# Router logits from the raw turned X of a two-layer MoE block, with the norm's factors folded into the router weights

## The chip, the cores and the metric

The kernel runs on one core of a Trainium2 chip. TensorE (PE) multiplies matrices, VectorE (DVE) and ScalarE (ACT) work on rows, GpSimd (POOL) and SyncE (SP) here mostly issue DMAs. The metric is the device time of one execution in microseconds (us), lower is better.

## The reference, cut to what matters

The whole program computes two layers of attention plus a hierarchical MoE (`first_block`), then a second block. All is float32. The part that the change touches stands between attention and the experts, once per layer:

```python
x = x + gt_a * (o @ w_o[i])                        # x: 256 rows; layer 0 also has 256 context rows xc
hf = _modulate(_rmsnorm(x, g_ffn[i]), sh_f, sc_f)  # h * (1 + scale) + shift
# _rmsnorm: x * rsqrt(mean(x*x) + eps) * g
# _hier_moe(tokens, ...):
p_grp = softmax(h @ w_group + b_group)             # 4 groups
lg = h @ w_router + b_router                       # 32 experts
# the best group, the best 2 of its 8 experts, and then the rows of h go to these experts
```

So 36 logits per token are wanted, and the rows h themselves, which the experts read.

## The kernel before, in words

A layer treats 4 tiles of 128 rows (layer 0: two of x, two of the context) or 2 (layer 1). `BATCHES` cuts them for the router: tiles (0, 1) and (2, 3) in layer 0, (0) and (1) in layer 1.

The loop after attention (`for tile in range(tiles)`, the W_o loop) does for each tile, in this order on PE: `wo_part` with column half 0 (8 products of 128x128 by 128x512; each is two matmul instructions in the trace, L1043), then for the tile before it `norm_turn` (8 transposes of its normed rows, L648) and, halfway through column half 1, `logits` (8 products with the 36 router columns `WRT`, L1053). DVE takes each half out with `out_part` (gate multiply L2269, add to X L2272). ACT makes the mean square and its root from the new X (`norm_sums`: L1420, L1422). DVE then makes the reciprocal (L1838) and the normed and modulated rows h (`modulated`: L1844, L1846). These rows `Hf` have two uses: POOL stores them to `h_d` in HBM (L2912), and PE turns them; ACT and DVE each copy one half of the turned tile into `HT` (L1409, L1851), from which `logits` reads.

When a batch's logits are there, DVE runs `route` (L1997 to L2025: top group, top two experts, counts), PE sums the counts (`positions`, L1061 and L1063), DVE makes slots and one-hot rows (`slots`, `map_rows`: L2042 to L2073), PE multiplies them into the slot map (`slot_map`, L787) and DVE hands the map over (`map_out`, L2079, a mark at L2081). POOL then gathers the first experts' input rows from `h_d` (L2925); it issues this gather behind waits for the map and for all stores of h (`s_hst`). PE turns them (L804) and the expert products start (L816).

Weights come through a ring of 6 slots of 2 MB, with one more slot in layer 0 and two more in layer 1, loaded by SP in a fixed order; each load waits until the last reader of its slot is done (L3037, L3035). Four facts of that order matter. The extra slot's first load (`in_w_up`) waits for the end of attention. Two loads wait for the two halves of w_o. The next (`in_w_gate`) takes the slot of the shift and scale rows, so it waits for the last `s_h`, which is what L1846 of the last tile counts up. All later ones wait for expert products.

ACT issues one DMA at the end of attention: the gains `g_ffn`, broadcast to 128 partitions (`VG`, L1517, 512 KB). DVE needs them for `scales` (L1814), after tile 0. All DMAs counted by `s_pre` are waited for together.

Of the kernel before, what the change touches and what calls it, by code (L numbers as in the profile page):

```python
# [110 lines left out]
def build(nc, t, out):  # L111

    ctx = ExitStack()
    with ctx:
# [3 lines left out]
        def sem(name):  # L118
            return ctx.enter_context(nc.semaphore(name))
# [68 lines left out]
        BRT = cut(20384, 36)  # L188
        SINK = cut(20424, HEADS)
        CROWS = cut(SCR, P, parts=7 * KD)  # L190

        STAGE = [cut(a, 512) for a in (21504, 21504, SCR, 21504, 21504, 21504)]
        QUADS = [(layer, c) for layer in range(2) for c in range(0, 12, 4)]
# [190 lines left out]
        s_silus = sem("silu_of_z")  # L384
        s_pos2 = sem("final_gain_and_positions")
        s_out = sem("out_stored")

        block = ctx.enter_context(nc.Block())

# [220 lines left out]
        def _(pe):  # L610
# [342 lines left out]
            def hT(tile, k):  # L953
                return HT[:, k, tile * P:(tile + 1) * P]

            for layer in range(2):
# [89 lines left out]
                def logits(tile):  # L1046
                    a, b = [x for x in BATCHES[layer] if x[0] <= tile < x[1]][0]
                    if tile == a:
                        pe.wait_ge(s_psd, so_far(s_ps))
                    pe.wait_ge(s_outA, turned[tile][0])  # L1050
                    pe.wait_ge(s_outD, turned[tile][1])
                    for k in range(KD):
                        ins = nc.tensor.matmul(banks[6][:, (tile - a) * 36:(tile - a) * 36 + 36], hT(tile, k), WRT[:, k, :],  # L1053
                                               start=(k == 0), stop=(k == KD - 1))
                    if tile == b - 1:
                        ins.then_inc(s_lg, 1)

                def positions(a, b):
# [7 lines left out]

                turned.clear()
                for tile in range(tiles):
                    pe.wait_ge(s_otaken, GROUPS_BEFORE[layer] + KV * (tile + 1))
                    u = unit("D")  # L1070
                    wo_part(u, tile, 0, range(KD)).then_inc(s_unitD, 1)
                    if tile == tiles - 1:
                        release(n0, "D")
                    early = batch_ending(layer, tile - 2)
                    if early:
                        positions(*early)
                    if tile:
                        norm_turn(tile - 1, Hf[(tile - 1) % 2])
                        turned.append((count["A"], count["D"]))
                    u = unit("D")  # L1080
                    wo_part(u, tile, 1, range(KD // 2))
                    if tile:
                        logits(tile - 1)
                    wo_part(u, tile, 1, range(KD // 2, KD)).then_inc(s_unitD, 1)
                    if tile == tiles - 1:
                        release(n1, "D")
                early = batch_ending(layer, tiles - 2)
                if early:
                    positions(*early)
                norm_turn(tiles - 1, Hf[(tiles - 1) % 2])  # L1090
                turned.append((count["A"], count["D"]))
# [306 lines left out]
        def _(act):  # L1398
# [40 lines left out]
            def rows_to_ht(tiles):  # L1439
                for tile in tiles:  # L1440
                    u = take()
                    copy_out(HT[:, 0:4, tile * P:(tile + 1) * P], u[:, :].rearrange("p (k n) -> p k n", k=4))

            act.wait_ge(s_x, 16)
            for layer in range(2):
# [63 lines left out]
                for s in range(len(units) + 4):  # L1509
# [4 lines left out]
                    if 0 <= s - 1 < len(units):  # L1514
                        scaled(s - 1)
                act.wait_ge(s_o, GROUPS_AFTER[layer])
                act.dma_start(VG, t["g_ffn"][layer].partition_broadcast(P)).then_inc(s_pre, 16)  # L1517
                for tile in range(tiles):
                    if tile >= 1:
                        rows_to_ht([tile - 1])  # L1520
                    norm_sums([tile], X)
                rows_to_ht([tiles - 1])
# [217 lines left out]
        def _(dve):  # L1740
# [65 lines left out]

            def scales(layer, kinds):

                dve.wait_ge(s_pre, due(s_pre, 16))
# [25 lines left out]
            def modulated(layer, tile):  # L1835
# [4 lines left out]
                h = Hf[tile % 2]  # L1840
                if tile >= 2:
                    dve.wait_ge(s_hst[tile % 2], due(s_hst[tile % 2], 16))
                va, vb = ffn_rows(layer, tile // LAT)
                V.scalar_tensor_tensor(h, X(tile), rstd[:, tile:tile + 1], va, ALU.mult, ALU.mult).then_inc(s_v, one(s_v))  # L1844
                dve.wait_ge(s_v, so_far(s_v))
                V.tensor_tensor(h, h, vb, ALU.add).then_inc(s_h, one(s_h))  # L1846
                dve.wait_ge(s_h, so_far(s_h))

            def half_out(tile):
                u = take()  # L1850
                V.tensor_copy(HT[:, 4:8, tile * P:(tile + 1) * P], u[:, :].rearrange("p (k n) -> p k n", k=4)).then_inc(s_outD, one(s_outD))  # L1851

            def rope(tile, h0, h1, dst, tmp):

# [120 lines left out]
            def route(layer, a, b):  # L1975
# [9 lines left out]
                def first(dst, values, top, order, w, tmp):  # L1985
# [8 lines left out]
                    dve.wait_ge(s_v, so_far(s_v))  # L1994

                dve.wait_ge(s_lg, due(s_lg))
                V.tensor_tensor(lg, banks[6][:, 0:36 * n].rearrange("p (t e) -> p t e", t=n), bc(BRT.unsqueeze(1), P, n, 36),  # L1997
                                ALU.add).then_inc(s_v, one(s_v))
# [214 lines left out]
            for layer in range(2):  # L2213
# [51 lines left out]
                def out_part(tile, c):  # L2265
                    gate = GATE[tile // LAT]
                    cs = slice(c * 512, (c + 1) * 512)
                    u = take()
                    V.tensor_tensor(RES, u[:, :], gate[:, cs], ALU.mult).then_inc(s_outD, one(s_outD))  # L2269
                    dve.wait_ge(s_outD, so_far(s_outD))  # L2270
                    done = s_v if c == 0 else s_xr
# [3 lines left out]
                for tile in range(tiles):  # L2275
                    out_part(tile, 0)
                    early = batch_ending(layer, tile - 2)
                    if early:
                        slots(layer, *early)
                        map_rows(*early)  # L2280
                    if tile:
                        half_out(tile - 1)
                    done = batch_ending(layer, tile - 1)
                    if done:
                        route(layer, *done)
                    out_part(tile, 1)
                    if tile == tiles - 1:
                        V.memset(mark(), 0.0).then_inc(s_par_free, one(s_par_free))
                    if tile == 0:
                        scales(layer, tiles // LAT)  # L2290
# [4 lines left out]
                early = batch_ending(layer, tiles - 2)  # L2295
                if early:
                    slots(layer, *early)
                    map_rows(*early)
                half_out(tiles - 1)
                route(layer, *BATCHES[layer][1])  # L2300
# [847 lines left out]
```

## Time and profile before

| | |
|---|---|
| three runs | 2111.34 us median (2108.47 to 2114.01) |
| profiled execution | 2110.83 us, of which the span is 2109.0 us |
| PE busy | 1971.9 us (93% of the span) |
| DVE, ACT, POOL busy | 1062.7, 405.5, 118.9 us |
| DMA | 584.23 MB, mean 277 GB/s |
| chain that ended last | PE 76%, DMA 13%, DVE 8%, ACT 2% |

The page's strips show PE nearly full from end to end, with two dips in which also the granted clock of PE falls, one after each W_o loop. Times in the rows below are from the span's start. The first number of a timeline row is its start and the second its length; the bracket at its end is how long the engine was idle before it and what ended that.

### The profile page before, as it was taken

The numbers are of one execution on the slowest core, as the hardware profiler recorded it, in microseconds if no ns is written. First come the engines' busy times: TensorE is split into PE (matmuls) and PEld (weight loads), VectorE is DVE, ScalarE is ACT, GpSimd is POOL, SyncE is SP. The second block draws the span as 40 slices with busy tenths as digits, with TensorE's granted clock in tenths as the row PEclk, the third lists the DMA queues.
The fourth block names the chain that finished last, engine by engine and source line by source line (L and its number), as shares of the span: only waits on it lengthen the run. The fifth ranks groups of instructions, "written<-read, shape, count | busy, mean of one in ns | idle before, by whom it ended". The sixth has DMA issues, their size and how long they took to land.

```text
span 2109.0 us, 20648 instructions
## 1 busy us (share of the span) xinstructions
PE 1971.9 (93%) x8057; PEld 888.9 (42%) x8057; DVE 1062.7 (50%) x1974; ACT 405.5 (19%) x836; POOL 118.9 (6%) x168
## 2 busy tenths in 40 slices
PE   6999987999999999988799988898999999999999
PEld 2445443333333333454333333333445554445554
DVE  1257545445554445674433222322767665666665
ACT  2146411000000002162100000000312230212230
POOL 1001002000000000000100000000100000100000
PEclk9999997999999999999799999999999999999999
DMA  9267435999999998455599999999733333723431
GB/s 356 98 232 264 184 127 223 416 425 426 427 427 427 426 427 329 173 210 188 220 425 426 427 425 427 425 426 424 268 114 120 120 120 120 255 101 115 140 134 65
DMA packets 95043, 584.23 MB, mean 277 GB/s; under 512 B 10044, under 2 KB 14436, under 8 KB 62044
## 3 DMA queue, kind: packets, MB, share of 16 engines
q1 hardware_dynamic: 84400, 559.96, 65.7%
q0 software_dynamic: 10256, 21.86, 3.1%
q8 instruction: 67, 1.10, 0.2%
q10 hardware_dynamic: 288, 1.05, 0.2%
q14 instruction: 32, 0.26, 0.0%
HBM read 589.05 MB, written 4.26 MB: 281 GB/s over the span
## 4 chain that ended last, share of the span: by engine, by line
PE 76%; DMA 13%; DVE 8%; ACT 2%; SPq 1%; issue 1%; DVEq 0%; POOLq 0%; ACTq 0%
PE bank L816 25%; PE bank L1144 11%; PE bank L821 6%; DMA ring<-in_w_gate 6%; PE bank L975 6%; DMA ring<-in_w_up 4%; PE bank L1223 4%; PE bank L1159 3%; PE bank L1120 3%; PE bank L1043 2%; PE bank L766 2%; PE bank L663 2%; PE bank L754 2%; PE bank L804 1%; DMA ring<-in_w_qkv 1%
## 5 line engine op out<-in xcount | busy, mean ns | idle before, releaser
L816 PE MATMUL bank<-ring,big 128*64 128x512 f32 x2464 | 684.7, 602 | 25.7 <-DMA ring<-in_w_gate 10.0
L816 PEld LDWEIGHTS bank<-ring,big 128*64 128x64 f32 x2464 | 217.7, 138 | 387.3 <-issue 374.2
L2165 DVE TENSOR_TENSOR big<-bank,big 128x512 f32<-128x512 f32 x192 | 131.6, 685 | 252.3 <-PE bank L821 251.5
L816 PE MATMUL bank<-big 128*64 128x512 f32 x512 | 227.5, 594 | 0.0
L1144 PE MATMUL bank<-ring,big 128*128 128x512 f32 (+1 forms) x448 | 205.3, 600 | 5.3 <-DVE ring L2548 3.3
L821 PE MATMUL bank<-big 128*128 128x512 f32 x360 | 180.1, 610 | 0.0
L975 PE MATMUL bank<-ring,big 128*128 128x512 f32 x320 | 141.8, 602 | 3.8 <-ACT big L1435 2.0
L1144 PEld LDWEIGHTS bank<-ring,big 128*128 128x128 f32 x448 | 82.6, 193 | 93.9 <-issue 92.8
L2369 DVE TENSOR_TENSOR big<-big,bank 128x512 f32<-128x512 f32 x32 | 22.0, 687 | 184.5 <-PE bank L816 184.5
L975 PEld LDWEIGHTS bank<-ring,big 128*128 128x128 f32 x320 | 61.2, 193 | 80.0 <-issue 74.7
L816 PEld LDWEIGHTS bank<-big 128*64 128x64 f32 x512 | 68.6, 137 | 58.9 <-issue 58.9
L821 PEld LDWEIGHTS bank<-big 128*128 128x128 f32 x360 | 59.4, 191 | 78.3 <-issue 78.3
L2170 DVE TENSOR_TENSOR xl<-xl,big 128x512 f32<-128x512 f32 x128 | 88.7, 693 | 4.4
L1529 ACT ACTIVATE big<-bank 128x512 f32<-128x512 f32 x32 | 19.1, 597 | 362.3 <-PE bank L804 362.3
L1223 PE MATMUL bank<-ring,big 128*128 128x512 f32 x192 | 83.6, 593 | 1.5 <-ACT big L1409 1.5
L1409 ACT ACTIVATE big<-bank 128x512 f32<-128x512 f32 (+2 forms) x66 | 36.3, 568 | 252.5 <-PE bank L975 115.8
L1043 PE MATMUL bank<-ring,big 128*128 128x512 f32 x192 | 84.6, 595 | 0.0
L1561 ACT ACTIVATE big<-bank 128x512 f32<-128x512 f32 x32 | 19.1, 597 | 326.2 <-PE bank L816 326.2
L1144 PE MATMUL bank<-ring 128*128 128x512 f32 (+1 forms) x176 | 79.2, 590 | 0.0
L2386 DVE COPY big<-bank 128x512 f32<-128x512 f32 x32 | 22.1, 692 | 106.7 <-PE bank L816 106.7
L2920 POOL MEMSET big<- 128x1024 f32 x32 | 30.3, 952 | 678.4 <-PE bank L804 666.9
L663 PE MATMUL bank<-ring,small 128*32 128x512 f32 x384 | 54.1, 657 | 7.5 <-DMA ring<-in_w_ada 7.5
(443 smaller groups left out, 2380.8 us busy)
## 6 DMA issues: line engine op xcount, KB each, us to landing
ring<-in_w_gate SPq DMA_DIRECT2D x52, 2048.0 KB, 17.9
ring<-in_w_up SPq DMA_DIRECT2D x51, 2048.0 KB, 21.2
ring<-in_w_down SPq DMA_DIRECT2D x51, 2048.0 KB, 20.5
ring<-in_w_ada SPq DMA_DIRECT2D x24, 2048.0 KB, 10.4
ring<-in_w_in SPq DMA_DIRECT2D x24, 2048.0 KB, 7.9
big<-in_w_up SPq DMA_DIRECT2D x9, 2048.0 KB, 21.3
big<-in_w_down SPq DMA_DIRECT2D x9, 2048.0 KB, 21.6
big<-in_w_gate SPq DMA_DIRECT2D x8, 2048.0 KB, 19.2
```

The lines of the kernel that those rows point to most:

```text
L663: ins = nc.tensor.matmul(u[32 * i:32 * i + 32, :], cW[:, 2 * k:2 * k + 32], w[:, (4 * (k % 2) + i) * 512:(4 * (k % 2) + i + 1) * 512], sta ...
L754: ins = nc.tensor.transpose(banks[4 + r][:, o * P:(o + 1) * P], src, ident)
L816: ins = nc.tensor.matmul(bank[half * CAP:(half + 1) * CAP, :], lhs[:, k, half * CAP:(half + 1) * CAP], slot_cols(slots[half], k * step + c ...
L821: return nc.tensor.matmul(bank, OHW[layer][j][:, (u // 2) * P:(u // 2 + 1) * P], YS[j][:, (u % 2) * 512:(u % 2 + 1) * 512], start=True, st ...
L975: ins = nc.tensor.matmul(u[:, :], hT(tile, k), w[:, k, :], start=(k == 0), stop=(k == KD - 1))
L1043: ins = nc.tensor.matmul(u[:, :], hT(tile, k), wo[c][:, k, :], start=(k == 0), stop=(k == KD - 1))
L1120: ins = nc.tensor.matmul(u[:, 0:cols], HT2[:, k, tile * P:(tile + 1) * P], w[:, 0:KD * cols].rearrange("p (k n) -> p k n", k=KD)[:, k, :], ...
L1144: ins = nc.tensor.matmul(u[:, 0:cols], a[:, k, :], b[:, k, :], start=(k == 0 and (name not in ADDS_TO or (g in (IN_PAIRS, FIRST) and name ...
L1159: ins = nc.tensor.matmul(u[:, 0:n], HT2[:, k, tile * P:(tile + 1) * P], w[:, k, :], start=(k == 0), stop=(k == KD - 1))
L1223: ins = nc.tensor.matmul(u[:, :], YT[n % 2][:, k, tile * P:(tile + 1) * P], w[:, k, c * 512:(c + 1) * 512], start=(k == 0), stop=(k == 3))
L2165: return r, V.tensor_tensor(r, bank, GATE[tile // LAT][:, half * 512:(half + 1) * 512], ALU.mult)
L2170: return V.tensor_tensor(x, x, r, ALU.add)
```

## The change

X itself is turned, not h. With X the updated rows, r their reciprocal root, the logits are r * (X @ M) + B, where M is W with each row multiplied by g * (1 + scale), and B is shift @ W + bias.

- ACT issues small DMAs ahead of `VG`: the shift and scale rows of each stream (2 streams in layer 0) as 16 rows of 128, and g_ffn as 8 rows of 128. They count on `s_pre` as `VG` does.
- PE, in tile 0 after 4 of the 8 steps of unit 0, waits for all DMAs on `s_pre` and turns these rows (`columns_turn`). It then makes shift @ W (`shift_product`) and spreads it over the partitions (`shift_rows`); ACT copies each out.
- DVE makes M (`router_weights`) and B (`router_bias`) during tile 0.
- PE turns X of the tile before after 2 steps of unit 0 (`x_turn`) and makes its logits after 6. Of the last tile the first half is turned inside unit 1, the second behind it.
- ACT copies both halves of the turned tile.
- `route` begins with one multiply-add of PSUM, r and B per tile.
- The last tile's h is finished (`shifted_rows`, the adding of the shift, which counts `s_h`) behind the last `route`. In layer 1 `slots` of batch 0 stands ahead of the last `out_part`.

```diff
@@ PE
+                def columns_turn():
+                    pe.wait_ge(s_pre, due(s_pre, 16 * (2 + streams)))
+                    n = 16 * streams + KD
+                    nc.tensor.transpose(unit("A")[:, 0:n], MROWS[0:n, :], ident[0:n, 0:n]).then_inc(s_unitA, 1)
...
+                def shift_product():
+                    pe.wait_ge(s_outA, count["A"])
...
+                        ins = nc.tensor.matmul(u[0:36, 0:streams], WRT[:, k, :], MCOL[:, k:k + 16 * streams:16], start=(k == 0), stop=(k == KD - 1))
...
+                def x_turn(tile, half):
...
+                        ins = nc.tensor.transpose(u[:, k * P:(k + 1) * P], X(tile)[:, c:c + P], ident)
...
-                    wo_part(u, tile, 0, range(KD)).then_inc(s_unitD, 1)
...
+                    if tile == 0:
+                        wo_part(u, tile, 0, range(4))
+                        columns_turn()
+                        wo_part(u, tile, 0, range(4, KD)).then_inc(s_unitD, 1)
+                        shift_product()
+                    else:
+                        wo_part(u, tile, 0, range(2))
+                        pe.wait_ge(s_xr, X_BEFORE + tile)
+                        x_turn(tile - 1, 0)
+                        x_turn(tile - 1, 1)
+                        wo_part(u, tile, 0, range(2, 6))
+                        logits(tile - 1)
+                        wo_part(u, tile, 0, range(6, KD)).then_inc(s_unitD, 1)
...
+                    wo_part(u, tile, 1, range(4))
+                    if tile == 0:
+                        shift_rows()
+                    if final:
+                        pe.wait_ge(s_xh, layer + 1)
+                        x_turn(tile, 0)
+                    wo_part(u, tile, 1, range(4, 7))
+                    if final and batch_ending(layer, tiles - 2):
+                        positions(*batch_ending(layer, tiles - 2))
+                    wo_part(u, tile, 1, range(7, KD)).then_inc(s_unitD, 1)
...
-                norm_turn(tiles - 1, Hf[(tiles - 1) % 2])
-                logits(tiles - 1)
+                logits(tiles - 1, 0)
+                pe.wait_ge(s_xr, X_BEFORE + tiles)
+                x_turn(tiles - 1, 1)
+                logits(tiles - 1, 1)
@@ ACT
+                act.wait_ge(s_mod, (128, 256)[layer])
+                for s in range(streams):
+                    act.dma_start(MROWS[16 * s:16 * s + 16, :], mod_d[layer, s, 3 * D:5 * D].rearrange("(k p) -> k p", p=P)).then_inc(s_pre, 16)
+                act.dma_start(MROWS[16 * streams:16 * streams + KD, :], t["g_ffn"][layer].rearrange("(k p) -> k p", p=P)).then_inc(s_pre, 16)
                 act.dma_start(VG, t["g_ffn"][layer].partition_broadcast(P)).then_inc(s_pre, 16)
...
+                    if tile == tiles - 1:
+                        rows_to_ht(tile, 0)
+                    act.wait_ge(s_xr, due(s_xr))
+                    nc.scalar.activation(junk[:, :], X(tile), ACT.Square, accum_out=ss[:, tile:tile + 1]).then_inc(s_a, one(s_a))
+                    if tile == tiles - 1:
+                        rows_to_ht(tile, 1)
+                    act.wait_ge(s_a, so_far(s_a))
+                    nc.scalar.activation(ss[:, tile:tile + 1], ss[:, tile:tile + 1], ACT.Sqrt, scale=1.0 / D, bias=eps).then_inc(s_ss, 1)
@@ DVE
+                for tile in range(a, b):
+                    bias = BRM[:, 36 * (tile // LAT):36 * (tile // LAT) + 36]
+                    ins = V.scalar_tensor_tensor(LG[:, tile, :], banks[6][:, 36 * (tile - a):36 * (tile - a) + 36], rstd[:, tile:tile + 1], bias,
+                                                 ALU.mult, ALU.add)
...
-                    modulated(layer, tile)
+                    if between:
+                        map_rows(*between)
+                    scaled_rows(layer, tile)
+                    if not final:
+                        shifted_rows(layer, tile)
+                route(layer, *BATCHES[layer][1])
+                shifted_rows(layer, tiles - 1)
                 last_use[at["rows", layer]] = (s_h, so_far(s_h))
```

First place: ACT at the end of layer 0's attention (`big<-in_g_ffn 128x1024` is `VG`). Before:

```order
L1482 ACTIVATE big<-bank 128x2x256 x2
L1517 DMA big<-in_g_ffn 128x1024
L1420 ACTIVATE junk,small<-xl 128x1024
L1422 ACT_TABLE_LOAD
L1422 ACTIVATE small<-small 128x1
```

Now:

```order
L1535 ACTIVATE big<-bank 128x2x256 x2
L1573 DMA big<-mod_d 16x128 x2
L1574 DMA big<-in_g_ffn 8x128
L1575 DMA big<-in_g_ffn 128x1024
L1463 ACTIVATE big<-bank 128x40
L1463 ACTIVATE big<-bank 36x2
L1463 ACTIVATE big<-bank 128x72
L1584 ACTIVATE junk,small<-xl 128x1024
```

`VG` is now the fourth DMA on ACT instead of the first (the third in layer 1), and three copies out of PSUM stand ahead of the first square.

Second place: PE at the head of the same W_o loop (`wo_part` is L1043 before and L1047 now). Before:

```order
L766 MATMUL bank<-big 64x256 x8
L1043 MATMUL bank<-ring,big 128x512 x24
L648 MATMUL bank<-cst,big 128x128 x8
L1043 MATMUL bank<-ring,big 128x512 x4
L1053 MATMUL bank<-big 128x36 x8
```

Now:

```order
L770 MATMUL bank<-big 64x256 x8
L1047 MATMUL bank<-ring,big 128x512 x4
L1056 MATMUL bank<-cst,big 128x40
L1047 MATMUL bank<-ring,big 128x512 x4
L1064 MATMUL bank<-big 36x2 x8
L1047 MATMUL bank<-ring,big 128x512 x4
L1072 MATMUL bank<-cst,big 128x36 x2
L1047 MATMUL bank<-ring,big 128x512 x6
L1081 MATMUL bank<-cst,xl 128x128 x8
```

L1056 waits for the four ACT DMAs and has only 4 steps of W_o ahead of it; 24 unbroken steps became 4, 4, 4 and 6 until the first tile is turned.

Third place: DVE behind the last update of X in layer 0. Before:

```order
L2272 TENSOR_TENSOR xc<-xc,big 128x512
L2288 MEMSET small 128x1
L1838 RECIPROCAL small<-small 128x1
L1844 SCALAR_TENSOR_TENSOR big<-xc,small,ring 128x1024
L1846 TENSOR_TENSOR big<-big,ring 128x1024
L1851 COPY big<-bank 128x4x128
L1997 TENSOR_TENSOR big<-bank,big 128x72
```

Now (ahead of the route's rows, and behind them):

```order
L2363 TENSOR_TENSOR xc<-xc,big 128x512
L2381 MEMSET small 128x1
L1907 RECIPROCAL small<-small 128x1
L1912 SCALAR_TENSOR_TENSOR big<-xc,small,ring 128x1024
L2087 SCALAR_TENSOR_TENSOR big<-bank,small,big 128x36 x2
...
L2116 TENSOR_TENSOR big<-big 128x32 x2
L1918 TENSOR_TENSOR big<-big,ring 128x1024
L2133 TENSOR_TENSOR big<-bank,cst 128x64
```

The copy out of PSUM is gone, and the add that finishes h moved from ahead of the route to behind it.

## Rows read from the trace of the kernel before

**Rows 1.** Windows: busy us of PE, PEld, DVE, ACT, POOL; clock; DMA share; GB/s
```profile
238.00:305.00 67.00, 64.42 (x210) 32.57 (x206) 30.71 (x68) 7.41 (x13) 1.65 (x3) 1.00 0.26 95
500.00:600.00 100.00, 100.00 (x420) 37.91 (x418) 50.41 (x75) 8.37 (x14) 7.78 (x8) 1.00 1.01 427
1200.00:1300.00 100.00, 88.10 (x392) 34.65 (x389) 28.18 (x44) 7.53 (x13) 6.18 (x7) 1.00 1.01 425
```

**Rows 2.** Timeline of layer 0's W_o loop and of what follows its last unit
```profile
238.52 20.87 PE L1043 MATMUL bank<-ring,big 128*128 128x512 f32 x48
...
264.12 1.87 PE L1053 MATMUL bank<-big 128*128 128x36 f32 x16
...
299.89 1.95 PE L1053 MATMUL bank<-big 128*128 128x36 f32 x16 [1.60 <-DVE big L1851]
...
305.38 0.69 DVE L2269 TENSOR_TENSOR big<-bank,big 128x512 f32<-128x512 f32 x1 [5.64 <-PE bank L1043]
...
308.01 0.29 ACT L1422 ACTIVATE small<-small 128x1 f32<-128x1 f32 x1
...
309.86 1.22 DVE L1846 TENSOR_TENSOR big<-big,ring 128x1024 f32<-128x1024 f32 x1
...
311.14 1.97 PE L648 MATMUL bank<-cst,big 128*128 128x128 f32 x8 [5.79 <-DVE big L1846]
...
317.69 0.23 DVE L1997 TENSOR_TENSOR big<-bank,big 128x72 f32<-128x72 f32 x1 [3.79 <-PE bank L1053]
```

**Rows 3.** Timeline of layer 0 from the end of the last route to the gather
```profile
323.50 0.74 PE L1061 MATMUL bank<-big,cst 128*128 128x96 f32 x2 [4.16 <-DVE big L2025]
...
331.02 0.06 DVE L2081 MEMSET small<- 128x1 f32 x1
...
332.01 1.06 POOL L2925 DMA_INDIRECT big<-h_d,slot_tok  x1 [12.45 <-DVE small L2081]
```

**Rows 4.** DMAs at the end of layer 0's attention; then KB, us to landing
```profile
238.62 0.38 ACTq L1517 DMA_DIRECT2D big<-in_g_ffn  x1
239.12 0.33 SPq L3037 DMA_DIRECT2D big<-in_w_up  x1
...
big<-in_w_up SPq DMA_DIRECT2D x1, 2048.0 KB, 9.1
big<-in_g_ffn ACTq DMA_DIRECT2D x1, 512.0 KB, 4.5
```

**Rows 5.** PE after a wait of 4 us in layer 1's attention, and that window
```profile
898.71 1.11 PE L985 MATMUL bank<-cst,big 128*128 128x128 f32 x4 [4.00 <-DVE big L1882]
...
896.00:904.00 8.00, 4.46 (x20) 2.18 (x20) 4.12 (x9) 1.49 (x2) 0.00 (x0) 0.57 1.01 380
```

**Rows 6.** Stores of h: issue of layer 0's last, landings at 260, 311 and 1002
```profile
311.38 0.53 POOL L2912 DMA_DIRECT2D h_d<-big  x1 [16.85 <-DVE big L1846]
...
h_d<-big POOLq DMA_DIRECT2D x1, 512.0 KB, 2.9
...
h_d<-big POOLq DMA_DIRECT2D x1, 512.0 KB, 9.5
...
h_d<-big POOLq DMA_DIRECT2D x1, 512.0 KB, 9.8
```

**Rows 7.** Layer 1: the DMAs at attention's end, the last unit, route and gather
```profile
963.51 0.34 ACTq L1517 DMA_DIRECT2D big<-in_g_ffn  x1
964.00 0.33 SPq L3037 DMA_DIRECT2D big<-in_w_up  x1
...
995.60 0.69 DVE L2269 TENSOR_TENSOR big<-bank,big 128x512 f32<-128x512 f32 x1
...
1008.86 0.20 DVE L1997 TENSOR_TENSOR big<-bank,big 128x36 f32<-128x36 f32 x1 [3.78 <-PE bank L1053]
...
1013.95 0.69 PE L1061 MATMUL bank<-big,cst 128*128 128x64 f32 x2 [4.29 <-DVE big L2025]
...
1020.70 1.08 POOL L2925 DMA_INDIRECT big<-h_d,slot_tok  x1 [9.97 <-DVE small L2081]
```

More of the change, by code:

```diff
@@ L190, in build @@
         CROWS = cut(SCR, P, parts=7 * KD)
+        WRM = [cut(4096 + 288 * s, 288, KD, 36) for s in range(2)]
+        MROWS, MCOL = cut(4672, P), cut(4800, 40)
+        BCOL, BRM = cut(4840, 2), cut(4844, 72)
         STAGE = [cut(a, 512) for a in (21504, 21504, SCR, 21504, 21504, 21504)]
@@ L1044, in wo_part @@
                     return ins
-                def logits(tile):
+                streams = tiles // LAT
+                def columns_turn():
+                    pe.wait_ge(s_pre, due(s_pre, 16 * (2 + streams)))
+                    n = 16 * streams + KD
+                    nc.tensor.transpose(unit("A")[:, 0:n], MROWS[0:n, :], ident[0:n, 0:n]).then_inc(s_unitA, 1)
+                    marks["columns", layer] = count["A"]
+                def shift_product():
+                    pe.wait_ge(s_outA, count["A"])
+                    u = unit("A")
+                    for k in range(KD):
+                        ins = nc.tensor.matmul(u[0:36, 0:streams], WRT[:, k, :], MCOL[:, k:k + 16 * streams:16], start=(k == 0), stop=(k == KD - 1))
+                    ins.then_inc(s_unitA, 1)
@@ new lines, in shift_rows @@
+                def shift_rows():
+                    pe.wait_ge(s_outA, count["A"])
+                    u = unit("A")
+                    for s in range(streams):
+                        ins = nc.tensor.matmul(u[:, 36 * s:36 * s + 36], BCOL[0:36, s:s + 1].to_broadcast([36, P]), ident[0:36, 0:36],
+                                               start=True, stop=True)
+                    ins.then_inc(s_unitA, 1)
+                def x_turn(tile, half):
+                    u = unit("A")
+                    for k in range(4):
+                        c = (4 * half + k) * P
+                        ins = nc.tensor.transpose(u[:, k * P:(k + 1) * P], X(tile)[:, c:c + P], ident)
+                    ins.then_inc(s_unitA, 1)
+                    turned.append(count["A"])
@@ L1047, in logits @@
+                X_BEFORE = (NT, 3 * NT)[layer]
+                def logits(tile, half=None):
                     a, b = [x for x in BATCHES[layer] if x[0] <= tile < x[1]][0]
-                    if tile == a:
+                    if tile == a and half != 1:
                         pe.wait_ge(s_psd, so_far(s_ps))
[L1050 to L1053, printed above, removed]
+                    pe.wait_ge(s_outA, turned[2 * tile + (0 if half == 0 else 1)])
+                    for k in range(KD) if half is None else range(4 * half, 4 * half + 4):
+                        ins = nc.tensor.matmul(banks[6][:, (tile - a) * 36:(tile - a) * 36 + 36], hT(tile, k), WRM[tile // LAT][:, k, :],
@@ L1054, in logits @@
                                                start=(k == 0), stop=(k == KD - 1))
-                    if tile == b - 1:
+                    if tile == b - 1 and half != 0:
                         ins.then_inc(s_lg, 1)
@@ L1437, in modulated_to_ht, with rows_to_ht @@
                     ins.then_inc(s_outA, 1)
[L1439 to L1442, printed above, removed]
+            def rows_to_ht(tile, half):
+                u = take()
+                copy_out(HT[:, 4 * half:4 * half + 4, tile * P:(tile + 1) * P], u[:, :].rearrange("p (k n) -> p k n", k=4))
             act.wait_ge(s_x, 16)
@@ L1833, in modulated_half, with scaled_rows @@
                 ins.then_inc(s_outD, one(s_outD))
-            def modulated(layer, tile):
+            def scaled_rows(layer, tile):
                 dve.wait_ge(s_ss, due(s_ss))
@@ L2275, in _ @@
                 for tile in range(tiles):
+                    final = tile == tiles - 1
+                    if batch_ending(layer, tile - 2):
+                        slots(layer, *batch_ending(layer, tile - 2))
+                        map_rows(*batch_ending(layer, tile - 2))
                     out_part(tile, 0)
[L2277 to L2285, printed above, removed]
+                    if tile == 0:
+                        router_weights(layer, tiles // LAT)
+                    if batch_ending(layer, tile - 1):
+                        route(layer, *batch_ending(layer, tile - 1))
+                    between = final and batch_ending(layer, tiles - 2)
+                    if between:
+                        slots(layer, *between)
                     out_part(tile, 1)
-                    if tile == tiles - 1:
+                    if final:
                         V.memset(mark(), 0.0).then_inc(s_par_free, one(s_par_free))
                     if tile == 0:
+                        router_bias(layer, tiles // LAT)
                         scales(layer, tiles // LAT)
@@ L2292, in _ @@
                             dve.wait_ge(s_mod, 128)
-                    modulated(layer, tile)
-                last_use[at["rows", layer]] = (s_h, so_far(s_h))
[L2295 to L2300, printed above, removed]
+                    if between:
+                        map_rows(*between)
[4 more added lines that the diff above has]
+                shifted_rows(layer, tiles - 1)
+                last_use[at["rows", layer]] = (s_h, so_far(s_h))
                 slots(layer, *BATCHES[layer][1])
```

71 lines of the change are left out of this document (40 added, 31 removed).

## Prediction

> **What bounds the kernel now.** I read the windows first, to see which engine fills each stage. In layer 0's W_o loop PE is busy 64.42 of 67 us at full clock [rows 1], so there whatever PE does more, or waits for, is paid. In the expert stages PE is busy for the whole of a window of layer 0 at 427 GB/s, and 88 of 100 us in layer 1 at 425 GB/s, where the DMAs pace it [rows 1]. Both stages start from the same point: the ring is full, the next load waits for the first expert product, and that waits for the gather. So the expert stages, bound by PE or by DMA, move as a block with the gather, and what the change is worth is read from two moments, the gather at 332.01 [rows 3] and the one at 1020.70 [rows 7].
>
> Then the timeline up to each gather. W_o costs 20.87/48 = 0.435 us an instruction, and logits 1.87 us a tile [rows 2]. After the last unit of layer 0 the work is one chain: last half taken (305.38), square and root (308.01), reciprocal and h (309.86 to 311.08), transposes at half clock, copy, logits, route at 317.69 [rows 2]. That is 12.3 us. In layer 1 the same stretch is 995.60 to 1008.86, 13.3 us [rows 7]. The route and the slot map follow, and the gather comes 8.5 us after the last route's end (323.50 to 332.01) and 6.75 us in layer 1 [rows 3, 7].
>
> **The part that helps: the tail.** After the last half is taken at time e, X is complete at e+1.45. ACT's square still ends at about e+2.6 as before (the root started 2.63 after e [rows 2]). PE turns the second half meanwhile, so ACT's copy of it (0.6, as for its other copies) runs e+2.6 to e+3.2 and the root ends at e+3.55. DVE's reciprocal and first multiply take the 1.55 us that before lay between the root's end (308.30) and L1846 (309.86) [rows 2], to e+5.1. The remaining half of the logits ends at about e+4.3. So route starts at e+5.1, plus 0.1 in layer 0 for one instruction more. Gain: 7.1 us in layer 0, 8.2 in layer 1. The add that finishes h moved behind route costs nothing by itself towards the map: it takes 1.22 us [rows 2] beside the positions that DVE waits for (323.50 to 324.7, [rows 3]).
>
> **The part that costs: the W_o loop.**
> - New products. 16 instructions of shift @ W, priced between nearly nothing and the logits' 0.117 each (1.87/16, [rows 2]), which take wider weights: I take 1.2 us. Spreading and the column transpose: 0.5. Layer 0 1.7 us, layer 1 1.5.
> - The first half of the last tile's transposes moves into the loop: 0.5 us.
> - In layer 0 the stalls go, of which the 1.60 before L1053 is the largest [rows 2]. All are 67 less 64.42 us, or 2.6 [rows 1]. I leave 0.3 for `positions`: gain 2.3. In layer 1 `positions` (0.4) comes inside unit 1 and `slots` (about 1.4 us) ahead of the last take, which starts 0.7 us late for it. Against the route that held the last take before (by 1.2 us), this and the two lines above make +1.6.
> - The wait for the ACT DMAs. PE reaches `columns_turn` 8 instructions in, at 238.52 + 3.5 = 242.0. `VG` alone, issued first, landed 4.5 us after 238.62, at 243.1 [rows 4]. Now three small DMAs stand ahead of it at 0.38 us each, so it is issued at 239.8, behind SP's 2 MB of w_up at 239.12 [rows 4]. Two bounds. If it still lands in 4.5 us: 244.3, wait 2.3. If it shares with w_up as the stores of h do when a 2 MB load goes out beside them (9.5 and 9.8 against 2.9 us alone; all four that met a load took 8.7 to 9.8 [rows 6]): w_up, which had `VG` ahead of it, landed at 248.2 [rows 4], and the two are the same bytes in either order, so `VG` lands by about 248.2, wait 6.2. I take this one. One of those four stores was issued a little before its load (the 9.8) and still came late; `VG` goes out 0.7 us after its load. In layer 1 PE gets there at 966.9, `VG` is issued at 964.3, 0.3 us behind w_up's 964.00 [rows 7] and with 2 MB of w_down right behind that: between 968.9 and 978, I take 974, wait 7.1.
> - The clock after such a wait. After 4.00 us idle PE made four transposes in 1.11 us, where eight take that at full speed, and the window around it shows 0.57 [rows 5]: the 1.2 GHz level for about 7 us. After the 1.60 us idle it stayed at 2.4 GHz (1.95 for the logits [rows 2]). For waits of 6 to 7 us I take a slow stretch of 3.4 us beyond the wait, 1.7 us lost in each layer. Bounds 0 and 3.4.
>
> The row says that whichever transfer is first goes nearly first: w_up, for all that it is 2 MB, did not slow `VG` before. 
>
> **The part that undoes the gain: the store of the last h.** The last `s_h` releases two things at once: POOL's store of the last tile and SP's `in_w_gate` load. Before, that was 311.1; the store went out at 311.38 and landed at 320.9 [rows 6], 11 us before the gather at 332.01 [rows 3], and nobody saw it. Now `s_h` comes behind route, 1.25 us after its end. Store 0.3 later, landing 9.5 (it still meets the load, since both wait for the same count; if it didn't: 2.9), and then the 0.85 us that POOL needs from a release to the gather (0.93 behind DVE's mark [rows 3]). From route's end: 1.25 + 0.3 + 9.5 + 0.85 = 11.9 us, against 8.5 by way of the map. So the store takes over the gather, at 3.4 us in layer 0. In layer 1 by the same sum with 9.3: 11.7 against 6.75, 4.95 us. Behind the store in POOL's queue stand only the gate loads, the zeroing and the gather; the gather is what PE waits for.
>
> **The sum.** Layer 0: wait 6.2 + clock 1.7 + products 1.7 + half turn 0.5 - stalls 2.3 = +7.8 at the last unit; tail -7.1; so route ends 0.7 late; store +3.4: the gather is 4.1 us later. Layer 1: wait 7.1 + clock 1.7 + 1.6 = +10.4; tail -8.2; route ends 2.2 late; store +4.95: 7.1 later. Together +11.2 us. On the profiled execution (span 2109.0, with 1.8 around it 2110.83) that is 2122.0; the median of the runs shown, 2111.34, lies half a us above it, which I leave.
>
> **The rivals.**
> 1. `VG` is on time. ACT's ring gets its turn beside SP's, as it had before, and lands 4.5 us after issue. Waits 2.3 and 2.0, no slow clock. Layer 0: 4.1 - 3.9 - 1.7 = -1.5; layer 1: 7.1 - 5.1 - 1.7 = +0.3. Time 2109.6, not slower. For it: `VG` landed in 4.5 and 4.6 us with w_up going out 0.5 us later. Against: then it was first.
> 2. The store is not in the way: it lands in 2.9 us, or soon enough. `VG` late, though. Layer 0 +0.7, layer 1 +2.2: 2113.7. For it: 2.9 us at 260. Against: no load met that one, and here the load waits for the very same event. It decides from a landing of 6.1 us after issue in layer 0 and 4.4 in layer 1.
> 3. Both go well. Layer 0: +0.7 - 3.9 - 1.7 = -4.9; layer 1: +2.2 - 6.8 = -4.6: 2101.3, faster. This is what the change would give if only its tail counted; it needs both of the above.
> 4. Both waits at their worst: `VG` lands with the last of w_down in layer 1 (978, +4) and the slow clock lasts twice as long in both (+3.4): 2129.4.
> That the change does not shorten the tail at all is hardly open: PE waited 5.79 us for h [rows 2], and X is ready 4.2 us before h.
>
> **How the numbers follow.** Forecast (both transfers late, with its spread from small terms of 3 us either way) 0.57, rival 4 0.05, rival 1 0.18, rival 2 0.10, rival 3 0.10. A measurement of this kernel can tell about 0.3%, or 6.3 us, from no change: under 2105.0 is faster, over 2117.7 slower. Faster: rival 3 and a little of rival 1, 0.12. Slower: the forecast but for its low edge, and rival 4, 0.58. The same: the rest, 0.30. Predicted 2122. The range reaches down past rival 1 to 2107 and up to 2128, which leaves out rival 3 and most of rival 4. The likeliest case's own range is 2117 to 2126.
>
> **What would show it.** An idle of 6 us on PE before the 128x40 transpose, put down to a DMA, and half clock behind it; then a late `VG` is right, with 2 us rival 1 is. The last half's take in layer 0 at about 313. Route 5.1 to 5.2 us after that take. The last store issued about 1.5 us after route's end, landing 9 us later, with the gather right behind it and no longer behind DVE's mark; a gather 8.5 us after route's end shows rival 2. The forecast is wrong if either transfer lands in under 5 us, and if the expert stages do not keep their length.

## The result and the profile after

The changed kernel took 2126.25 us (median of 4 runs, 2122.61 to 2128.38) against 2112.68 for the kernel before, timed beside it (4 runs): ratio 1.0056, interval 1.0042 to 1.0070, so slower by a little over half a per cent, and clear of the noise. Its profiled execution took 2122.61 us, the lowest of the four, with a span of 2120.8, 11.8 more than before.

Layer 0 first: the start of the W_o loop on PE with the DMAs of ACT and SP, in the timeline of the kernel after. These rows answer to [rows 2] and [rows 4].

```profile
237.82 3.70 PE L1047 MATMUL bank<-ring,big 128*128 128x512 f32 x8
237.92 0.83 ACTq L1573 DMA_DIRECT2D big<-mod_d  x2
238.43 0.33 SPq L3131 DMA_DIRECT2D big<-in_w_up  x1
238.79 0.66 ACTq L1574 DMA_DIRECT2D big<-in_g_ffn  x1
239.48 0.37 ACTq L1575 DMA_DIRECT2D big<-in_g_ffn  x1
247.56 0.33 PE L1056 MATMUL bank<-cst,big 40*128 40x40 f32 x1 [6.04 <-DMA big<-in_g_ffn]
247.81 6.09 PE L1047 MATMUL bank<-ring,big 128*128 128x512 f32 x8
253.83 0.72 PE L1064 MATMUL bank<-big 128*36 128x2 f32 x16
```

PE does 8 instructions of W_o and then stands still for 6.04 us until the last ACT DMA is there. Eight instructions of the same kind took 3.70 us ahead of the wait and take 6.09 behind it. The windows of the two stretches behind the wait (columns as in [rows 1]) show a mean granted clock of 0.61, so mostly the 1.2 GHz level, and then 2.4 GHz again:

```profile
247.80:254.00 6.20, 6.20 (x14) 2.55 (x14) 0.00 (x0) 0.20 (x1) 0.00 (x0) 0.61 0.01 3
254.00:260.00 6.00, 6.00 (x31) 3.10 (x30) 2.45 (x6) 0.40 (x2) 0.00 (x0) 1.00 0.00 0
```

Next the end of the loop and the way to the gather, in the timeline of the same kernel; it answers to [rows 2], [rows 3] and [rows 6].

```profile
313.45 0.69 DVE L2360 TENSOR_TENSOR big<-bank,big 128x512 f32<-128x512 f32 x1 [5.96 <-PE bank L1047]
...
316.43 0.28 ACT L1588 ACTIVATE small<-small 128x1 f32<-128x1 f32 x1
...
316.94 1.28 DVE L1912 SCALAR_TENSOR_TENSOR big<-xc,small,ring 128x1024 f32<-128x1024 f32 x1
318.15 0.41 DVE L2087 SCALAR_TENSOR_TENSOR big<-bank,small,big 128x36 f32<-128x36 f32 x2
...
323.65 1.23 DVE L1918 TENSOR_TENSOR big<-big,ring 128x1024 f32<-128x1024 f32 x1
...
324.90 0.33 SPq L3131 DMA_DIRECT2D ring<-in_w_gate  x1
...
325.17 0.53 POOL L3006 DMA_DIRECT2D h_d<-big  x1 [22.86 <-DVE big L1918]
...
326.74 1.86 POOL L3014 MEMSET big<- 128x1024 f32 x2
...
326.98 0.25 DVE L2154 TENSOR_REDUCE big<-big 128x4 f32<-128x96 f32 x1
...
327.26 1.37 DVE L2156 TENSOR_SCALAR big<-big 128x4 f32<-128x4 f32 x1
...
332.40 0.06 DVE L2172 MEMSET small<- 128x1 f32 x1
...
335.75 1.06 POOL L3019 DMA_INDIRECT big<-h_d,slot_tok  x1 [7.15 <-DMA h_d<-big]
```

The tail is short now: the last half is taken at 313.45 and the route starts at 318.15, 4.7 us later instead of 12.3. But the add that finishes h (L1918) ends at 324.88, the store of h and the 2 MB load of `in_w_gate` leave together behind it, and the gather's bracket names the store. DVE's mark (L2172) was there 3.3 us before the gather. The DMA view of the same stretch gives KB and us to landing:

```profile
ring<-in_w_gate SPq DMA_DIRECT2D x1, 2048.0 KB, 9.3
h_d<-big POOLq DMA_DIRECT2D x1, 512.0 KB, 9.7
```

Layer 1 repeats it. These timeline rows answer to [rows 7]:

```profile
967.40 3.70 PE L1047 MATMUL bank<-ring,big 128*128 128x512 f32 x8
...
968.00 0.33 SPq L3131 DMA_DIRECT2D big<-in_w_up  x1
...
968.47 0.36 ACTq L1575 DMA_DIRECT2D big<-in_g_ffn  x1
...
978.50 0.30 PE L1056 MATMUL bank<-cst,big 24*128 24x24 f32 x1 [7.40 <-DMA big<-in_g_ffn]
978.73 5.86 PE L1047 MATMUL bank<-ring,big 128*128 128x512 f32 x8
...
1010.97 0.69 DVE L2360 TENSOR_TENSOR big<-bank,big 128x512 f32<-128x512 f32 x1
...
1016.07 0.25 DVE L2087 SCALAR_TENSOR_TENSOR big<-bank,small,big 128x36 f32<-128x36 f32 x1 [0.32 <-PE bank L1093]
...
1027.06 0.06 DVE L2172 MEMSET small<- 128x1 f32 x1
...
1032.19 1.08 POOL L3019 DMA_INDIRECT big<-h_d,slot_tok  x1 [7.60 <-DMA h_d<-big]
```

Counted from the start of each W_o loop (238.52 and about 963.4 before; 237.82 and 967.40 after), the last take is 8.8 us later in layer 0 and 11.4 in layer 1, and the gather 4.4 and 7.5 later. 4.4 + 7.5 = 11.9 is about the whole difference of the spans, 11.8. The expert stages kept their length: from layer 0's gather to the next W_o loop 631.7 us for 631.4 before, and from layer 1's gather to the end 1088.6 for 1088.3.

### The profile page after: what moved, and what is told of

The parts are those of the page before. It is cut to its first block, busy times and chain, and to the rows that moved or that the text cites. A ratio compares the mean times of both kernels' runs of the same rounds, so it can differ in the third digit from the quotient of the medians.

```text
span 2120.8 us, 20762 instructions
## 1 busy us (share of the span) xinstructions
PE 1977.5 (93%) x8097; PEld 889.5 (42%) x8097; DVE 1061.0 (50%) x1978; ACT 409.3 (19%) x848; POOL 119.0 (6%) x168
## 4 chain that ended last, share of the span: by engine, by line
PE 76%; DMA 14%; DVE 6%; ACT 1%; SPq 1%; issue 1%; ACTq 0%; DVEq 0%; POOLq 0%
PE bank L820 25%; PE bank L1198 11%; PE bank L825 6%; PE bank L979 6%; PE bank L1277 4%; PE bank L1047 3%; DMA big<-in_w_gate 3%; DMA ring<-in_w_gate 3%; DMA ring<-in_w_up 3%; PE bank L1213 3%; PE bank L1174 3%; PE bank L770 2%; PE bank L667 2%; PE bank L758 2%; DMA big<-in_w_up 2%; PE bank L808 1%
## 5 line engine op out<-in xcount | busy, mean ns | idle before, releaser
L979 PE MATMUL bank<-ring,big 128*128 128x512 f32 x320 | 140.6, 598 | 4.5 <-DMA ring<-in_w_qkv 2.4
L1463 ACT ACTIVATE big<-bank 128x512 f32<-128x512 f32 (+5 forms) x78 | 40.5, 540 | 293.5 <-PE bank L979 115.4
L1047 PE MATMUL bank<-ring,big 128*128 128x512 f32 x192 | 91.5, 625 | 0.0
L1277 PE MATMUL bank<-ring,big 128*128 128x512 f32 x192 | 83.6, 593 | 1.5 <-ACT big L1463 1.5
## 6 DMA issues: line engine op xcount, KB each, us to landing
ring<-in_w_ada SPq DMA_DIRECT2D x24, 2048.0 KB, 10.4
```

The lines of the kernel that those rows point to most:

```text
L979: ins = nc.tensor.matmul(u[:, :], hT(tile, k), w[:, k, :], start=(k == 0), stop=(k == KD - 1))
L1277: ins = nc.tensor.matmul(u[:, :], YT[n % 2][:, k, tile * P:(tile + 1) * P], w[:, k, c * 512:(c + 1) * 512], start=(k == 0), stop=(k == 3))
```

## The experiments

All were timed beside the kernel before, in two groups, each on one chip. For own count, gains first, gate load later and h ahead of the route the kernel before had a median of 2114.12 us in 27 runs; for the control, own count with later `in_w_up`, and the two last it had 2111.48 in 21. Ratios are to it, and kernels of different groups are compared by them.

**Small DMAs on a count of their own.** PE no longer waits for `VG`, only for the rows that it turns. The counter `s_c` stands at 7 DMAs by then, which is why the wait is for 10 and for 12. The order of issue is that of the changed kernel.

```diff
-                    pe.wait_ge(s_pre, due(s_pre, 16 * (2 + streams)))
+                    pe.wait_ge(s_c, 16 * (10, 12)[layer])
@@ ACT: the DMAs into MROWS
-.then_inc(s_pre, 16)
+.then_inc(s_c, 16)
@@ DVE, scales
-                dve.wait_ge(s_pre, due(s_pre, 16 * (2 + kinds)))
+                dve.wait_ge(s_pre, due(s_pre, 16))
```

> The changed kernel, but the small DMAs with the shift, scale and gain rows count on a semaphore of their own, and PE's columns_turn waits for these alone; the 512 KB of gains, still issued behind them, are waited for only by DVE's scales. Theory (the 512 KB come late because they are issued behind w_up, and PE waits for nothing else): the idle before the 128x40 and 128x24 transposes falls from 6.04 and 7.40 us to under 0.5, the half-clock stretches behind them (2.6 and 2.4 us lost) go too, 18 us in all: about 2108 where the changed kernel has 2126, so 4 to 5 us under the kernel before, ratio 0.998. Rival (the small DMAs themselves are slow, 16 rows of 512 bytes from HBM written shortly before): the idles stay above 4 us and the time stays above 2120.

Measured: 2111.96 us, ratio 0.9994 (0.9984 to 1.0004), span 2108.7. The timeline around PE's wait, layer 0 and layer 1:

```profile
239.19 0.66 ACTq L1574 DMA_DIRECT2D big<-in_g_ffn  x1
...
245.30 0.26 PE L1056 MATMUL bank<-cst,big 40*128 40x40 f32 x1 [3.38 <-DMA big<-in_g_ffn]
245.49 5.40 PE L1047 MATMUL bank<-ring,big 128*128 128x512 f32 x8
...
967.60 0.24 PE L1056 MATMUL bank<-cst,big 24*128 24x24 f32 x1
967.76 3.70 PE L1047 MATMUL bank<-ring,big 128*128 128x512 f32 x8
```

12 us came back, 10 of them between the two gathers (1032.19 became 1019.15, 335.75 became 332.49), where the wait and the slow clock are gone. In layer 0 the expectation of no wait failed: the one 4 KB transfer issued behind SP's `in_w_up` (238.83) held PE for 3.38 us, and the clock fell behind that wait: the mean granted clock from 245 to 251 was 0.72. So the kernel came 4 us above the 2108 expected. The gather is behind the store in both layers still.

**Gains first.** `VG` goes out ahead of the small DMAs, all on one count.

```diff
+                act.dma_start(VG, t["g_ffn"][layer].partition_broadcast(P)).then_inc(s_pre, 16)
                 act.wait_ge(s_mod, (128, 256)[layer])
...
-                act.dma_start(VG, t["g_ffn"][layer].partition_broadcast(P)).then_inc(s_pre, 16)
```

> The changed kernel, but ACT issues the 512 KB of gains first and the small row DMAs behind them; all count on one semaphore, and PE waits for all, as in the changed kernel. Theory (what is issued behind w_up waits for w_up's pieces, whatever its size): the small DMAs issued after w_up's 239.1 land late; PE still waits 3 to 6 us in each layer, time 2116 to 2124. Rival (bytes count: the 512 KB must share with w_up only if they come second): all land by about 243.5 and 968.5, PE waits 1 to 2 us, no slow clock, time about 2111 to 2113.

Measured: 2119.07 us, ratio 1.0021 (1.0011 to 1.0031), span 2115.2. The timeline around the waits:

```profile
246.72 0.32 PE L1056 MATMUL bank<-cst,big 40*128 40x40 f32 x1 [4.64 <-DMA big<-in_g_ffn]
246.97 6.28 PE L1047 MATMUL bank<-ring,big 128*128 128x512 f32 x8
...
973.71 0.24 PE L1056 MATMUL bank<-cst,big 24*128 24x24 f32 x1 [3.06 <-DMA big<-in_g_ffn]
973.87 3.70 PE L1047 MATMUL bank<-ring,big 128*128 128x512 f32 x8
```

The waits shrank to 4.64 and 3.06 us and did not vanish, though now only 4 and 8 KB transfers stand behind the 2 MB load. So place in the order decides first: whichever is issued behind `in_w_up` comes late. Bytes still count for something. The 4 KB released PE 6.9 and 5.8 us after their issue here and 6.1 with the own count, where the 512 KB issued behind the load took 8.1 and 10.0 to land (own count, layers 0 and 1).

**Gate load later.** In the changed kernel `in_w_gate` no longer waits for the last `s_h` but for the first expert transposes; the store of h goes out alone.

```diff
-                last_use[at["rows", layer]] = (s_h, so_far(s_h))
+                last_use[at["rows", layer]] = (expert_sems[layer][1], 1)
```

> The changed kernel, but SP's in_w_gate load into the slot of the shift and scale rows waits for the first expert transposes instead of the last s_h, so that it no longer goes out beside the last store of h. Theory (the store is late because it meets this load): the store lands in about 3 us instead of 9.7 and 9.1, and the gather follows DVE's mark by 0.95 us again: 2.4 us earlier in layer 0 and 4.1 in layer 1 than in the changed kernel, so about 2119.5 where that has 2126. The load is needed only by the second pair, some 25 us later, and costs nothing. Rival (the store is late of itself, by POOL's queue or the writing to HBM behind the route): it lands in 9 us still, time 2126.

Measured: 2118.31 us, ratio 1.0021 (1.0012 to 1.0031), span 2114.9. First its DMA view, then the timeline at the gather:

```profile
h_d<-big POOLq DMA_DIRECT2D x1, 512.0 KB, 3.0
```

```profile
331.81 0.06 DVE L2172 MEMSET small<- 128x1 f32 x1
...
332.80 1.06 POOL L3019 DMA_INDIRECT big<-h_d,slot_tok  x1 [4.78 <-DVE small L2172]
```

The store lands in 3.0 us instead of 9.7, and the gather is released by DVE's mark again. In layer 1 it lands in 3.7 instead of 9.1. The 2 MB load is what made the store late.

**Control.** The same edit in the kernel before, where the store has 11 us in hand in layer 0 and 9 in layer 1.

> A control: the kernel before, with the same edit of one load as in the run with the gate load later (in_w_gate waits for the first expert transposes). Theory (that run gained because the store had become the gather's bound): here the last store lands 11 us before the gather, so landing it 6 us earlier changes nothing: ratio 1.000, within 0.1%. Rival (the load beside it slows the gather, the route or the start of the experts in any kernel): a gain of 5 us or more here too, ratio 0.9975.

Measured: 2114.18 us, ratio 1.0011 (1.0001 to 1.0020), span 2110.5. The store landed in 3.5 and 3.0 us and the gather came as before behind the mark. Nothing gained, perhaps a tenth of a per cent lost. So the later gate load is worth something only where the store has become the bound.

The control's trace has one thing that the edit can't have caused, since it comes ahead of the first load that the edit moves. In the timeline of layer 0's W_o loop PE waits for DVE as it did before:

```profile
301.51 2.76 PE L1053 MATMUL bank<-big 128*128 128x36 f32 x16 [1.60 <-DVE big L1851]
304.08 6.25 PE L1043 MATMUL bank<-ring,big 128*128 128x512 f32 x8
```

Behind the same 1.60 us of waiting the logits took 1.95 us in the kernel before [rows 2] and its next 8 instructions of W_o 3.68. Here the mean granted clock from 302 to 306 is 0.55, and the last half is taken 70.2 us after the loop's start instead of 66.9. One execution of the same instructions can thus lose 3.4 us to the clock that another keeps.

**h finished ahead of the route.** The add of the shift stands ahead of the last `route` again, which sends the store some 5 us earlier.

```diff
                     scaled_rows(layer, tile)
-                    if not final:
-                        shifted_rows(layer, tile)
+                    shifted_rows(layer, tile)
                 route(layer, *BATCHES[layer][1])
-                shifted_rows(layer, tiles - 1)
```

> The changed kernel, but the last tile's shift is added ahead of the last route, as before the change. Theory: the store goes out 5 us earlier, meets w_gate as before and still lands before the gather is due; the route starts 1.25 us later, as the add stands before it, so the gather is by DVE's mark: 1.1 us earlier in layer 0 and 2.9 in layer 1 than in the changed kernel, about 2122 where that has 2126. Rival (the map, not the store, sets the gather): the 1.25 us are simply added twice, 2128.5.

Measured: 2122.40 us, ratio 1.0038 (1.0024 to 1.0052), span 2121.6. Its interval overlaps that of the changed kernel (1.0042 to 1.0070), so the timed runs don't tell the two apart, and the span of its profiled execution is not shorter. The gather is behind the mark in both layers, as it should be without the store. Counted from the start of its loop it comes after 97.9 us in layer 0, as in the changed kernel, and after 62.1 in layer 1 instead of 64.8. But the route of layer 0 took 7.64 us instead of 5.5. Its timeline has the reason:

```profile
323.40 2.27 DVE L2094 TENSOR_SCALAR big<-big 128x8 f32<-128x8 f32 x1
323.78 1.86 POOL L3012 MEMSET big<- 128x1024 f32 x2
```

A DVE operation of 8 columns, 0.17 us in the changed kernel, ends when POOL's two memsets do. They follow the store in POOL's queue and so moved into the route. This placing of the add gives back part of what it wins.

**Own count, and `in_w_up` behind the small rows.** SP's load of the extra slot waits until the rows for PE have landed (about 2.4 us).

```diff
                     sp.wait_ge(s_otaken, GROUPS_AFTER[name[1]])
+                    sp.wait_ge(s_c, 16 * (10, 12)[name[1]])
```

> As the run with an own count, and SP's loads into the extra slots (w_up first) wait for the small DMAs to land, so that nothing of SP is in front of them. Theory (even 4 KB wait behind w_up if issued behind it: 3.38 us of PE were left in layer 0 with the own count): the small DMAs land within 3 us of their issue, PE waits under 0.5 us in both layers, no slow clock in either loop, and w_up, some 2 us later, is not missed: 5 us less than the run with an own count, ratio to the kernel before 0.997. Rival (the small DMAs need 6 us by themselves in layer 0, where there are two streams): the wait of 3.4 us stays, ratio 0.9994.

Measured: 2106.95 us, ratio 0.9978 (0.9968 to 0.9987), span 2103.0. The timeline at PE's former wait, layer 0:

```profile
239.31 0.66 ACTq L1574 DMA_DIRECT2D big<-in_g_ffn  x1
...
240.85 0.33 SPq L3132 DMA_DIRECT2D big<-in_w_up  x1
241.97 0.26 PE L1056 MATMUL bank<-cst,big 40*128 40x40 f32 x1
242.16 3.70 PE L1047 MATMUL bank<-ring,big 128*128 128x512 f32 x8
```

No wait and no slow clock, and the last take comes 67.1 us after the loop's start (75.6 with the waits, 66.9 before the change). `VG` lands in 4.3 us. The gather is still released by the store (327.57). Against own count the profiled span is 5.7 us shorter; the intervals of the two ratios just touch (0.9984 to 1.0004 there).

**Both.** The last one with the later gate load.

> As the run before it, and in_w_gate waits for the first expert transposes. Theory (the two waits, for the gains and for the store, are all that stood against the shorter tail, and they add up): route ends 5 us earlier than before in both layers, the gather comes by DVE's mark in both, ratio 0.9935 to 0.9945, about 2101 where the kernel before has 2114. Rival (the expert stages, paced by DMA in layer 1, keep what comes earlier): ratio 0.997 or above.

Measured: 2099.54 us, ratio 0.9943 (0.9930 to 0.9956). The profiled execution was the slowest of the five (2103.04), span 2101.2. The stores land in 3.0 and 3.6 us, and in the timeline both gathers follow the mark:

```profile
325.60 1.06 POOL L3019 DMA_INDIRECT big<-h_d,slot_tok  x1 [4.77 <-DVE small L2172]
...
1011.21 1.08 POOL L3019 DMA_INDIRECT big<-h_d,slot_tok  x1 [3.43 <-DVE small L2172]
```

Counted from the start of each loop they come 6.4 us earlier than before in both layers, 12.8 together. The median has 11.9 of it; this one execution has 7.8, since its expert stages took 3.3 and 1.7 us longer than before, for a reason that stays open. One thing is left: L2156 takes 1.37 us beside POOL's memsets in layer 0.

**Zeroing earlier.** The same, with the two memsets issued ahead of the last store, as soon as the last logits are there.

```diff
                 for tile in range(tiles):
+                    if tile == tiles - 1:
+                        pool.wait_ge(s_lg, 2 * (layer + 1))
+                        G.memset(XE[0], 0.0).then_inc(s_xz, one(s_xz))
+                        G.memset(XE[1], 0.0).then_inc(s_xz, one(s_xz))
                     pool.wait_ge(s_h, (NT + NT) * layer + NT + tile + 1)
```

> As the run before it, and POOL zeroes the two gather targets ahead of the last store instead of behind it. Theory (a DVE tensor_scalar from SBUF to SBUF does not get through while POOL's memset runs: it took 1.37 us instead of 0.17 in the changed kernel's map rows, 2.27 in the route of the run with h before the route, each time until the memset's end): the long tensor_scalar in the map rows is back at 0.17, and the one in layer 1's route may be hit for under 1 us; 1 us less in layer 0, about 0 in layer 1, so the time moves by 0.05%, below what can be told; its trace tells. Rival (that instruction is long for another reason): it stays at 1.37.

Measured: 2097.42 us, ratio 0.9936 (0.9923 to 0.9949), span 2094.6. The timeline of layer 0:

```profile
309.96 0.95 POOL L3008 MEMSET big<- 128x1024 f32 x1
310.93 0.17 DVE L2094 TENSOR_SCALAR big<-big 128x8 f32<-128x8 f32 x1
...
318.62 0.17 DVE L2156 TENSOR_SCALAR big<-big 128x4 f32<-128x4 f32 x1
...
322.56 0.06 DVE L2172 MEMSET small<- 128x1 f32 x1
323.54 1.06 POOL L3023 DMA_INDIRECT big<-h_d,slot_tok  x1 [5.43 <-DVE small L2172]
```

L2156 is back at 0.17 us in layer 0; in layer 1 the memset now meets L2094 (0.62 us). This is the fastest kernel here, 13 us under the one before and about 25 under the changed one by the two ratios. Its step over the one above is not told apart by the timed runs, since the intervals overlap; the rows show it.

## Why the prediction was right

The forecast was 2122.0 and the kernel took 2126.25 in the median. Against the kernel before that was +13.6 us where +11.2 was predicted; the profiled executions differ by 11.8. The median lies a quarter of a us above the likeliest case's own range (2117 to 2126). It went by the forecast's own mechanism, term by term.

- **The wait for `VG`:** predicted 6.2 and 7.1 us, measured 6.04 and 7.40. That it comes late because it is issued behind `in_w_up` is what own count, gains first and `in_w_up` behind the rows show together; whether the two share or one queues behind the other, as the prediction has it both ways, no run separates. That `VG` would be in by the time at which `in_w_up` had landed was nearly right: with own count it landed at 239.88 + 8.1 = 248.0 and `in_w_up` at 247.2. By the rule cited from the Trainium skill (DMA: Bandwidth & Descriptors, Queues, rings and completion order) the pieces of that load would pass first, and the trace agrees with that. What the prediction made of it, that `VG` would land about 1 us ahead of `in_w_up`, does not follow if all of these pieces pass first, and it did not come: `VG` landed 0.8 us behind.
- **The clock:** 1.7 us a layer predicted, 6.09 - 3.70 = 2.4 and 5.86 - 3.70 = 2.2 measured on the first 8 instructions. Too low, inside the bounds of 0 and 3.4. Wait and clock together are what the loop costs: without both, the last take in layer 0 is 8.5 us earlier. That the clock stays up behind a wait of 1.60 us was read from one execution; in the control's it fell there, at a price of 3.4 us, and the forecast had no room for such a fall.
- **The rest of the loop:** the 16 products took 0.72 us where 1.2 was taken. But products, spreading and half turn, less the stalls that go, came to +0.2 us in layer 0 and +1.7 in layer 1, as the kernel without waits shows (`in_w_up` behind the rows), for -0.1 and +1.6 predicted. So the last take, at +8.8 and +11.4 for +7.8 and +10.4, is 1.0 us late in each layer, most of it the clock.
- **The tail:** 4.7 us from take to route in layer 0 where 5.2 was predicted: the root started 2.98 us after the take and not behind a full copy. In layer 1 it was 5.1 as predicted, but there the bracket of L2087 names PE's last logits and not the root. The route itself became 0.3 and 0.5 us shorter, which the forecast did not have: before, POOL's memsets ran beside it (317.72 and 1008.89) and one `tensor_scalar` in it (L2003) took 0.62 and 0.68 us instead of 0.17.
- **The store:** route's end to gather was 323.62 to 335.75, 12.1 us, for 11.9 predicted. The store landed 9.7 and 9.1 us after issue for 9.5 and 9.3. That this needs the gate load is shown by the 3.0 and 3.7 us without it, and that it bounds only the changed kernel by the control.
- **The sum at the gathers:** +4.4 and +7.5 for +4.1 and +7.1.

The rivals fell in the changed kernel, and the first three could be made; rival 4 was not tried. Rival 1, `VG` on time and the store late, was priced 1.2 us below the kernel before; with `in_w_up` behind the rows the median came 4.5 below, with no wait left where the rival kept 2.3 and 2.0 us. Rival 3, both transfers well, was priced at 2101.3; the kernel with both mended took 2099.54. It too had no wait, and it paid the 1.2 us of L2156, which no rival had. Rival 2 (store mended, `VG` late) was priced 2.9 us above the execution before; gate load later came 4.2 us above in the medians.

What the forecast missed is the memsets of POOL, which moved from beside the route to beside the slot map. In the changed kernel they cost nothing there, since the store is later than the mark anyway.

Left open: why the control is a tenth of a per cent slower (the fall of the clock is seen in its one profiled execution only), and how the delay of a transfer falls with the time by which it misses the big load's start. No run varied that time on its own.

## What to carry to other kernels

Where a small DMA gates an engine, look for a big one issued just ahead of it on another queue. Here the small one had to go first, or the big one to wait for it; whether it was 4 KB or 512 KB mattered less. When a change shortens one chain to a gather, look at the other condition of that gather and at what leaves at the same event, since here a load nobody was waiting for delayed the gathers by some 6 us in the two layers together. A reordering that looks bad as a whole can hold a gain: take the two waits away one at a time, and together.

## What the runs showed of the hardware that was not expected

- 4 KB, issued 0.36 us behind a 2 MB load of another queue, held PE until 6.1 us after its issue (239.19 to 245.30). Where the big load was made to wait for the small ones to land, the last of these had landed by 1.5 us after its issue (239.31), since the big load went out at 240.85.
- A DVE tensor_scalar from SBUF to SBUF waits for POOL's memsets: 128x4 took 1.37 us and ended at 328.63, as the second of two memsets did (326.74 + 1.86 = 328.60); 128x8 took 2.27 us with the add ahead of the route, where it began 0.38 us ahead of the first memset's recorded start, while POOL was issuing DMAs. A tensor_reduce that began under the same memsets (326.98) took 0.25. The Trainium skill (SBUF — State Buffer, Who interferes with whom) tells of this lock between `tensor_scalar` and GpSimd, held for one instruction; here DVE stood through the ends of both memsets.
- The clock after a wait: 3.38 and 4.64 us idle were followed by 8 instructions in 5.40 and 6.28 us, 6.04 by 6.09, 7.40 by 5.86, but 3.06 us idle in layer 1 (gains first) by 3.70, full speed. The length of the last wait alone does not decide it: behind 1.60 us the next 8 took 3.68 in the kernel before and 6.25 in the control.
